# The scan's old-state part goes to TensorE by an identity product, and the skip products and a second buffer move on GpSimd

## What is computed

```python
def ssd_chunked(xh, dt, A, bm, cm, h0):
    a_cum = jnp.cumsum(dt_c * A.reshape(G, R), axis=2)
    xdt = x * dt_c[..., None]
    decay = jnp.exp(jnp.where(lower, seg, -jnp.inf))       # seg = a_cum[i] - a_cum[j]
    cb = jnp.einsum('bcign,bcjgn->bcijg', Cc, Bc)
    y_diag = jnp.einsum('bcijg,bcijgr,bcjgrp->bcigrp', cb, decay, xdt)
    decay_to_end = jnp.exp(a_cum[:, :, -1:] - a_cum)
    states = jnp.einsum('bcjgn,bcjgr,bcjgrp->bcgrpn', Bc, decay_to_end, xdt)
    def step(h, inp):
        st, dcy = inp
        return h * dcy[..., None, None] + st, h
    h_final, h_in = lax.scan(step, h0, (states, chunk_decay))
    y_off = jnp.einsum('bcign,bcigr,cbgrpn->bcigrp', Cc, jnp.exp(a_cum), h_in)
    return y_diag + y_off, h_final
...
y = y_f + rev(y_b)                      # the two directions
y = y + d_skip[:, None] * xh            # the skip product
```

## Time and profile before

| | us |
|---|---|
| median of three runs | 3589.6 |
| lowest and highest | 3586.8, 3591.7 |
| the profiled execution | 3591.4 |
| its span, first to last instruction | 3589.6 |
| the scan's block in it | about 242 to 366 |

### The profile page before, as it was taken

The page is one execution under the profiler, slowest core; times in us unless marked ns, Lnnn a source line. Parts: engine busy times, 40 slices in busy tenths (PEclk is TensorE's granted clock), DMA queues, the critical chain, the costliest instruction groups (busy, mean ns, idle before and its releaser), DMA issues.

```text
span 3589.6 us, 36438 instructions
## 1 busy us (share of the span) xinstructions
PE 3301.5 (92%) x14474; PEld 2163.6 (60%) x14474; DVE 1232.4 (34%) x1764; ACT 991.3 (28%) x1713; POOL 283.3 (8%) x242
## 2 busy tenths in 40 slices
PE   6887999997899997999899989998998999989996
PEld 3546444444443442777577768876776577768874
DVE  3246121003101012454533453333454433543334
ACT  2126120002100001444533332222444533232212
POOL 0018020000100001021111000000011110000000
PEclk9998999998899999999999999999999999999998
DMA  6010343213699997111012312222311122222221
GB/s 230 0 71 1 141 164 117 71 47 130 274 409 409 409 409 279 59 59 49 30 59 71 97 63 95 95 83 79 85 59 49 36 65 75 96 70 94 90 82 63
DMA packets 265863, 436.63 MB, mean 122 GB/s; under 512 B 9312, under 2 KB 179808, under 8 KB 264928
## 3 DMA queue, kind: packets, MB, share of 16 engines
q1 hardware_dynamic: 265552, 432.41, 34.1%
q0 software_dynamic: 144, 1.90, 0.1%
HBM read 432.19 MB, written 2.10 MB: 121 GB/s over the span
## 4 chain that ended last, share of the span: by engine, by line
PE 52%; DVE 4%; ACT 2%; DVEq 1%; issue 1%; ACTq 0%; DMA 0%; POOLq 0%; SPq 0%; POOL 0%
PE bank L1966 43%; PE bank L2027 2%; PE bank L2044 1%; PE bank L2063 1%; PE bank L2003 1%; PE bank L1613 1%; DVE ring_r L2298 1%; ACT ring_r L2167 1%; PE bank L2058 1%; PE bank L2033 1%; DVE x L1644 0%; DVE layers_norm_rstd L1641 0%; DVE layers_work L2417 0%; DVE x_r L1655 0%; DMA ring<-in_w_in 0%
## 5 line engine op out<-in xcount | busy, mean ns | idle before, releaser
L1966 PE MATMUL bank<-experts_x_hi_r,ring_r 128*128 128x512 f32 x1720 | 576.6, 400 | 7.4 <-DVE ring_r L2298 7.4
L1966 PE MATMUL bank<-x_r,ring_r 128*128 128x512 f32 x1376 | 546.3, 397 | 0.0
L2298 DVE TENSOR_TENSOR ring_r<-ring,ring_r 128x2048 fp32r<-128x2048 f32 (+2 forms) x162 | 324.4, 2002 | 425.9 <-ACT ring_r L2167 425.0
L2167 ACT ACTIVATE ring_r<-ring 128x2048 fp32r<-128x2048 f32 (+2 forms) x162 | 272.7, 1683 | 494.1 <-PE bank L1966 475.0
L1966 PE MATMUL bank<-layers_work_r,ring_r 128*128 128x512 f32 x1312 | 391.2, 400 | 9.2 <-DVE layers_work_r L2441 9.2
L1966 PEld LDWEIGHTS bank<-experts_x_hi_r,ring_r 128*128 128x128 f32 x1720 | 324.3, 189 | 110.2 <-issue 25.2
L1966 PE MATMUL bank<-ring_r 128*128 128x512 f32 (+1 forms) x1224 | 387.9, 378 | 0.0
L1966 PEld LDWEIGHTS bank<-x_r,ring_r 128*128 128x128 f32 x1376 | 259.1, 188 | 62.7 <-issue 1.0
L1966 PEld LDWEIGHTS bank<-layers_work_r,ring_r 128*128 128x128 f32 x1312 | 248.6, 190 | 78.4 <-DVE layers_work_r L2441 10.1
L231 PE MATMUL bank<-xm,ring 128*128 128x512 f32 (+1 forms) x704 | 277.8, 554 | 0.9 <-DMA ring<-in_w_in 0.9
L2490 POOL TENSOR_TENSOR layers_p<-layers_p,layers_recip 128x512 f32<-128x512 f32 (+2 forms) x160 | 145.3, 925 | 1446.6 <-DVEq L2344 1446.6
(11 more groups left out here) (345 smaller groups left out, 4008.5 us busy)
## 6 DMA issues: line engine op xcount, KB each, us to landing
ring<-in_w_in SPq DMA_DIRECT2D x54, 1024.0 KB, 5.4
ring<-in_w_ffn_in SPq DMA_DIRECT2D x44, 1024.0 KB, 5.1
ring<-in_w_gate SPq DMA_DIRECT2D x30, 1024.0 KB, 18.4
ring<-in_w_down SPq DMA_DIRECT2D x28, 1024.0 KB, 18.5
ring<-in_w_in SPq DMA_DIRECT2D x13, 2048.0 KB, 12.2
ring<-in_w_up SPq DMA_DIRECT2D x26, 1024.0 KB, 18.1
mixer_kept<-in_w_down SPq DMA_DIRECT2D x24, 1024.0 KB, 18.5
mixer_kept<-in_w_up SPq DMA_DIRECT2D x23, 1024.0 KB, 18.2
```

What stands on the lines that cost most here:

```text
L1966: last = pe.matmul(out, lhs, rhs, start=start and k == 0, stop=stop and k == len(pairs) - 1)
L2167: act.activation(r32(whole(key, hi_at(i, key))), whole(key, raw_at(i, key)), ACT.Identity).then_inc(slab_round, 1)
L2298: dve.tensor_tensor(r32(tile), tile, r32(hi), ALU.subtract).then_inc(done, 1)
```

## The change

Five things, all in `scan`:

- `part` has one buffer, of its own. The old state's part is written there (L847 becomes L849), and a drain signals `part_done` behind it, before the diagonal products and not after them. The write waits for the second half of "diag" of the step before.
- On PE, each of the two halves of "diag" begins with a product of the 128x128 identity with 512 columns of `part` (128x512, new line L720), and the 16 products accumulate on it. The first identity product waits for `part_done`; `xdt` is waited for behind it.
- DVE adds the finished bank (diagonal and part) straight to the output `y` (L859, two halves), where it added it to the part. POOL's addition of the part to `y` (L883) is gone.
- POOL makes the skip products one at a time, behind the decays of steps 0 to 3 (L886), where all four stood ahead of the latent steps. DVE's first addition to `y` in these steps waits for them.
- The context steps' `xend` has two buffers: the second and fourth are written to `part`. So POOL waits for the "st" of two steps before, not of one.

```diff
-    part = [core.sb("part", [P, D], ctx)[:, :], a.xtok[:, TT, :]]
+    part = core.sb("part", [P, D], ctx)
+    xend_of = lambda u: (part if u < first and u % 2 else xend)[:, :]
...
-                pe.wait_ge(xdt_done, order[u] + 1)
+                pe.wait_ge(part_done, order[u] + 1)
                 for half in (0, 1):
                     core.banks.vacant(pe, ("diag", u, half))
+                    pe.matmul(core.ps(("diag", u, half))[:, :], core.c("ident"), part[:, half * 512:half * 512 + 512],
+                              start=True, stop=False)
+                    if half == 0:
+                        pe.wait_ge(xdt_done, order[u] + 1)
                     for g in (2 * half, 2 * half + 1):
...
-                                             start=True, stop=True)
+                                             start=False, stop=hd % 8 == 7)
...
-                mine = part[order[u] % 2]
-                if order[u] >= 2:
-                    dve.wait_ge(part_used, order[u] - 1)
-                if order[u] == 1:
-                    core.banks.filled(dve, ("st", first - 1, 1))
+                if order[u]:
+                    core.banks.filled(dve, ("diag", u - 1, 1))
                 for half in (0, 1):
                     core.banks.filled(dve, ("off", u, half))
-                    dve.tensor_tensor(by_head(mine)[:, 8 * half:8 * half + 8],
+                    dve.tensor_tensor(by_head(part[:, :])[:, 8 * half:8 * half + 8],
...
+                dve.drain().then_inc(part_done, 1)
+                for half in (0, 1):
+                    core.banks.filled(dve, ("diag", u, half))
+                    if half == 0 and order[u] < TT:
+                        dve.wait_ge(y_begun, order[u] + 1)
+                    dst = a.y[:, t, half * 512:half * 512 + 512]
+                    dve.tensor_tensor(dst, dst, core.ps(("diag", u, half))[:, :], ALU.add)\
+                       .then_inc(core.banks.done(("diag", u, half)), 1)
                 dve.drain()
...
-                if n:
-                    core.banks.filled(pool, ("st", feeds[n - 1], 1))
+                back = 2 if u < first else 1 if u > first else 2
+                if n >= back:
+                    core.banks.filled(pool, ("st", feeds[n - back], 1))
...
+            def begin_y(u):
                 t = steps[u][1]
-                pool.wait_ge(part_done, order[u] + 1)
-                if order[u]:
-                    pool.wait_ge(part_used, order[u])
-                pool.tensor_tensor(a.y[:, t, :], a.y[:, t, :], part[order[u] % 2], ALU.add).then_inc(part_used, 1)
+                pool.tensor_tensor(by_head(a.y[:, t, :]), by_head(a.xtok[:, t, :]), per_head(a.skip[:, :]), ALU.mult)\
+                    .then_inc(y_begun, 1)
...
                 decays(u)
-                if order[u]:
-                    add_part(u - 1)
-            add_part(outs[-1])
+                if order[u] < TT:
+                    begin_y(u)
```

More of the change, by code:

```diff
@@ L888, in _ @@
                 to_end(u)
-            for t in range(TT):
-                pool.tensor_tensor(by_head(a.y[:, t, :]), by_head(a.xtok[:, t, :]), per_head(a.skip[:, :]), ALU.mult)
-            pool.drain()
             pool.wait_ge(cb_done, 1)
             for u in outs:
-                t = steps[u][1]
                 if u in feeds:
```

13 lines of the change are left out of this document (3 added, 10 removed).

## The result

The changed kernel took 3599.7 us (median of 11 runs, 3598.1 to 3612.3) where the kernel before took 3591.2 (11 runs, 3586.8 to 3593.0). The ratio is 1.0031, 95% interval 1.0021 to 1.0040: the medians differ by 8.5 us, and the interval is 7.5 to 14.4. The forecast was 3592 and "within 0.2%". It was slower, by a little more than a measurement can tell. The profiled execution took 3598.8, with a span of 3597.0.

A forecast was written before the change was run, and what follows sets the result against it. PE's own work was taken to bound the mixer, so the scan's gain or loss passes on. Terms -7.2 + 7.9 + 6.4 - 4.5 = +2.6 on 3589.6 gave 3592 us, range 3583 to 3600.

The forecast's parts named there:

- within 0.2%: Whole kernel: a change of under 7.2 us, too small for a measurement to tell, chance 0.78.
- A: Start of step 0's diagonal block: begins at 272.8 in place of 280.0, -7.2 us; -9 if the clock is high.
- something else, such as ACT's decays: Sign of being wrong: step 0's block waits for another thing than the forecast named.
- B: Step 0's block to step 5's: identity products, longer waits and two low-clock stretches at 3.5 us each, +7.9 us.
- pauses of over 3 us: Sign of being right: PE's rows show idle time of over 3 us before L720, the identity product.
- Rival (1): Scan: the clock stays high, no low stretch in the loop; sum -6.2, 3583 us, chance 0.14.
- C: Steps 5 to 7 and last block: two periods 9.4 instead of 7.0, last block 1.6 longer, +6.4 us.
- Rival (2): Steps 1 to 5: pauses before identity products let the clock fall; from four falls, sum +13, 3602 us, chance 0.14.
- D: End of scan: POOL's last addition gone, pause before the mixer shorter, its first products at full clock, -4.5 us.
- What the scan's block gains or loses is handed on: Scan to mixer: the mixer's length is PE's own, so the scan's shift passes on to what follows.
- Slower: Whole kernel over 3596.8 us, the outcome given to the rival of repeated clock falls, chance 0.14.

The follow-up runs named there:

- the start alone: Kernel before, with two buffers for the context steps' xend and the skip products behind the decays of steps 0 to 3: 3580.9 us, ratio 0.9973.
- the fillers: Changed kernel with two more 128x512 products a step among the sums, results overwritten, to hold PE's clock up: 3605.2 us, ratio 1.0040.

## Why the prediction was wrong

**A, the start, -7.2: right, in part by luck.** Measured -7.4 (38.04 to 30.69); the kernel with the start alone is 9.5 us faster. The main mechanism is the one named: xend no longer waits for the skip products, and it is done 8.3 us earlier, counted from the scan's first product, where I had 7.6. The way from there to the block isn't. xend held up DVE's xdt (2.97 us) and not the other way round; "st" ran at full clock (1.89), for which I had given -9; and the block began behind PE's own sums, the last of them held by ACT, and not behind the part. That way took 6.7 us for 6.1. I had named "something else, such as ACT's decays" as a sign of being wrong, and for this block it was so.

**B, steps 0 to 5, +7.9: right in size.** Measured +7.4. Two falls, in steps 1 and 3, as assumed; those periods are 16.5 and 15.9, the others 13.4, 13.9 and 12.2, against 13.7 and 12.1 forecast. But pauses of over 3 us, forecast before every identity product, stand only before steps 1 and 3. The kernel with the clock held up shows what this agreement is worth: no fall, periods of 14.2, since the fillers use the time. What the falls cost alone can't be taken from it. (Rival (1) let the identity products more than double a block's columns; 2 of 512 beside 16 of 64 just double them.)

**C, steps 5 to 7 and the last block, +6.4: this step failed.** Measured 8.4 for the two periods and 1.7 for the block, +10.1. The period at full clock is right: 9.1, where 9.4 was forecast. But I had counted falls in steps 0 to 5 alone and put none in C, while the pause before step 5's block, 2.10 us, has the same chain behind it as the ones ahead of it: it ends B, and what its fall costs lies in C. The block took 9.4 us, the period 13.2: 3.8 over the forecast. Rival (2) named such a fall, but only together with four in B; a case with two there and one here was missing. The trace of before had a warning that I left out, for my list of its pauses had 2.72 and 2.95 (fall) and 2.35 and 0.82 (none), but not the one of step 4:

```profile
330.28 6.35 PE L724 MATMUL bank<-scan_xdt,scan_seg 128*128 128x64 f32 x32 [2.28 <-issue]
```

A pause of 2.28 was followed by the low clock and one of 2.35 was not. So the pause's length alone doesn't decide it, and 2.10 was no reason to expect none. Without the identity products the clock fell in the last block behind a pause of 0.83 and did not in step 5 behind 1.25.

**D, the end, -4.5: right, with 1.0 more.** The pause went from 3.81 to 1.27 and the 64 records from 30.6 to 27.6: -5.5. I had counted the five slow records of the earlier trace rows alone; the low stretch went on for 2 us behind them. In one of five profiles the clock did fall there (29.3), and in the kernel with the fillers too.

**Sum in the scan: +2.6 forecast, +4.6 measured.** The experiments cut it another way, in the scan's time of one profile each (that of before differs by 0.5 between its two profiles, that of after by 0.5 among five):

| from, to | us |
|---|---|
| before, start alone | 154.7 to 145.3, -9.3 |
| start alone, then no addition of the part at all (output incomplete), `y` written by DVE | to 138.9, -6.4 |
| PE waits for the part | to 150.0, +11.1 |
| identity products | to 159.3, +9.3 |

Leaving the addition out altogether is worth 6.4 us, and making it on PE costs 20.4. The 6.4 is more than any complete kernel had: with the addition on POOL the scan took 145.1, as the start alone. The split into 11.1 and 9.3 holds in this order only, as the kernel with the identity products last shows. My text had the wait's price nowhere as one number: in B it was in the second half of L847 and a drain, in C in the chain. The profile of before couldn't show it for steps 1 to 5, for there PE waits for the bank of "off", that is, for nearly the same moment.

**Behind the scan: 0 forecast, +2.3 to +4.8 measured: the second failure.** "What the scan's block gains or loses is handed on" leaves this out: the unchanged part is itself of another length in each kernel, and of these 2 us and more are the rows near 1440, where before itself is the exception. That the clock goes with it is seen for the stretch at 1430 to 1470 only; the cause of the other places was not looked for. Why 7 of 22 timed runs of after are some 8 us longer stays open, since no profile caught one. The kernel with the fillers, profiled at 3612.3, had a fall in its last block and the longest stages behind the scan of all; this may be the same thing, but it isn't shown.

So the step that failed inside the scan is C, at 6.4 where 10.1 was measured: the third fall. In the sum A, B and D gave 1.7 of these 3.7 us back. The rest of the way from my 3592 to 3600, at the edge of the range, is 2 to 5 us behind the scan, and 1.6 by which the median of before came out higher in the comparison (3591.2) than the one I started from (3589.6). "Slower" had 0.14 because I tied it to a fourth fall and took nothing for the unchanged part.

The Trainium skill, "SBUF — State Buffer", section "Who interferes with whom", says that a DVE instruction with both inputs in SBUF and a GpSimd instruction that reads SBUF exclude each other. The trace agrees: DVE's L809 above took 2.92 us beside POOL's skip product and its L815, with one input in PSUM and a row of POOL beside it as well, took 1.29 for its two halves as in the earlier trace rows.

## What to carry to other kernels

Before work is moved from an engine off the path to the one that sets it, ask what the critical engine must newly wait for: here the products cost some 9 us and the wait for their operand up to 11, more than the 6 that leaving the addition out altogether gave. Split a change that has parts: its start alone is 3580.9 us, 0.27% faster than before, and no complete kernel that was tried beats it by a measurable amount. Where a clock falls in pauses, count the falls in every step of the loop, the last ones too, and allow some us for unchanged stages behind it.

## What the runs showed that I had not expected

- The falls repeat: five profiles of one kernel, on at least two chips, have them in the same steps, with periods equal within 0.2 us, and two profiles of before differ by 0.1 us over the 3193 us behind the scan. Between kernels the same code there took 3191.1 to 3202.4 us. But the loop of before had other falls in its second profile (periods 12.3, 10.4, 14.7 where the first has 11.1, 14.6, 13.9), so it isn't one pattern for each kernel.
- Wide products pay part of their own price: 13.8 us of identity products cost 8 to 10, while the clock in the window went from 0.77 to 0.86.
- A full clock is not by itself a shorter loop: at 1.00 with no pause on PE the periods were 14.2 us, and at 0.79 to 0.82 the kernels without identity products had 11 to 14.
